# The second one-hot of the expert gates: four small ScalarE squares with the key as bias, where GpSimd subtracted and ScalarE squared once

## The reference, cut to what matters

```
v1, i1 = top_k(s[:, :, 0], 16);  v2, i2 = top_k(s[:, :, 1], 16)     # 8 heads, 128 keys on each side
vals, sel = top_k(v1[:, None] + v2[None, :], 16)
e1 = i1[sel // 16];  e2 = i2[sel % 16];  eid = e1 * 128 + e2         # 8 * 16 = 128 picks of a token
gate = softmax(vals)
w = gate * gelu(u[eid] . h);   y = sum over the picks of w * v[eid]
```

## Time and profile before

| | before |
|---|---|
| median of three runs | 2830.35 us (2830.07 to 2835.6) |
| profiled execution | 2832.78 us, of which the span of its instructions is 2831.2 us |
| mean granted clock of TensorE, whole span | 0.937 |
| gate loop of layer 0 | about 797.7 to 966.9 us, 169.2 us |
| gate loop of layer 1 | about 2227.5 to 2394.4 us, 166.9 us |
| VectorE busy in these loops | 160.24 and 161.08 us |
| ScalarE busy in these loops | 103.92 and 83.20 us |
| GpSimd busy in these loops | 77.41 and 76.91 us |
| granted clock in these loops | 0.94 and 0.80 |

### The profile page before, as it was taken

One profiled execution on the slowest core, in us unless ns is written; L12 is line 12 of the kernel. 1 busy time (PEld: TensorE's weight loads), 2 busy tenths in 40 slices (PEclk: granted clock), 3 DMA queues, 4 the chain that ended last, 5 costly groups with the idle time before them and its releaser, 6 DMA issues.

```text
span 2831.2 us, 55687 instructions
## 1 busy us (share of the span) xinstructions
PE 2554.8 (90%) x17972; PEld 2403.6 (85%) x17972; DVE 1794.1 (63%) x4076; ACT 1349.0 (48%) x2491; POOL 184.4 (7%) x201
## 2 busy tenths in 40 slices
PE   6986899999987899999796968999999867999996
PEld 3964899999965699999796858999999756999996
DVE  2435569884479755555546875588844798555554
ACT  2512445555556554545454223455556554555553
POOL 1000000000034200000000000000000243000000
PEclk7987999999999999999898878999999978999998
DMA  6444334444444354444342104344444200544442
GB/s 240 164 170 175 133 139 156 163 148 170 157 163 148 136 185 163 163 166 167 122 163 75 60 37 143 135 162 163 148 163 163 82 0 23 180 164 167 165 163 83
DMA packets 108412, 401.05 MB, mean 142 GB/s; under 512 B 12384, under 2 KB 12528, under 8 KB 107200
## 3 DMA queue, kind: packets, MB, share of 16 engines
q1 hardware_dynamic: 103104, 375.44, 37.9%
q0 software_dynamic: 5248, 24.88, 2.4%
HBM read 389.62 MB, written 10.65 MB: 141 GB/s over the span
## 4 chain that ended last, share of the span: by engine, by line
PE 79%; DVE 14%; issue 3%; DMA 2%; ACT 1%; DVEq 1%; SPq 0%; POOL 0%; ACTq 0%; POOLq 0%
PE ps L1186 22%; PE ps L1188 22%; PE ps L1187 22%; PE ps L1412 4%; DVE onehot L1092 3%; DMA raw<-in_ada_w 2%; PE ps L1215 1%; DVE spl L662 1%; PE ps L1332 1%; DVE big L1098 1%; PE ps L1348 1%; PE ps L1361 1%; DVE big L834 1%; PE ps L1251 1%; DVE big L1043 1%
## 5 line engine op out<-in xcount | busy, mean ns | idle before, releaser
L1186 PE MATMUL ps<-hs,spl 128*128 128x288 f32 x4960 | 1480.7, 299 | 78.3 <-DVE hs L714 46.0
L1187 PE MATMUL ps<-hs,spl 128*128 128x288 f32 x4960 | 1472.0, 297 | 0.0
L1188 PE MATMUL ps<-hs,spl 128*128 128x288 f32 x4960 | 1469.5, 296 | 0.0
L662 DVE TENSOR_TENSOR spl<-raw,spl 128x512 fp32r<-128x512 f32 x1240 | 843.4, 690 | 831.7 <-ACT spl L424 829.3
L424 ACT ACTIVATE spl<-raw 128x512 fp32r<-128x512 f32 x1240 | 772.9, 630 | 630.1 <-PE ps L1188 627.4
L1186 PEld LDWEIGHTS ps<-hs,spl 128*128 128x128 f32 x4960 | 939.0, 189 | 91.9 <-issue 60.5
L1188 PEld LDWEIGHTS ps<-hs,spl 128*128 128x128 f32 x4960 | 942.1, 190 | 0.0
L1187 PEld LDWEIGHTS ps<-hs,spl 128*128 128x128 f32 x4960 | 940.6, 190 | 0.0
L1412 PE MATMUL ps<-hs,onehot 128*128 128x128 f32 x1152 | 212.3, 333 | 91.1 <-DVE onehot L1092 65.6
L1412 PEld LDWEIGHTS ps<-hs,onehot 128*128 128x128 f32 x1152 | 175.3, 227 | 132.3 <-issue 58.2
L1092 DVE TENSOR_SCALAR onehot<-iota,choice 128x128 f32<-128x128 f32 x576 | 240.1, 480 | 5.5 <-PEq L1401 4.4
(11 more groups left out here) (223 smaller groups left out, 1282.5 us busy)
## 6 DMA issues: line engine op xcount, KB each, us to landing
raw<-in_peer_u SPq DMA_DIRECT2D x256, 512.0 KB, 3.2
raw<-in_peer_v SPq DMA_DIRECT2D x256, 512.0 KB, 3.2
raw<-in_ada_w SPq DMA_DIRECT2D x96, 512.0 KB, 5.2
raw<-in_peer_wq SPq DMA_DIRECT2D x32, 512.0 KB, 3.2
raw<-in_hg_w_in SPq DMA_DIRECT2D x32, 512.0 KB, 3.3
raw<-in_ab_w_in SPq DMA_DIRECT2D x28, 512.0 KB, 3.3
raw<-in_ab_w_out SPq DMA_DIRECT2D x8, 512.0 KB, 6.1
big<-in_state_hgrn POOLq DMA_DIRECT2D x8, 512.0 KB, 3.8
```

Of the source, the lines that this page charges most:

```text
L662: dve.tensor_tensor(spl[:, slot % 2, 1, cols], raw[:, slot, cols], spl[:, slot % 2, 0, cols].bitcast(F32), ALU.subtract).then_inc(low_read ...
L1186: pe.matmul(out, spl[:, slot, 0, cols], high, start=start, stop=False, skip_group_check=True)
L1187: pe.matmul(out, spl[:, slot, 0, cols], low, start=False, stop=False, skip_group_check=True)
L1188: return pe.matmul(out, spl[:, slot, 1, cols], high, start=False, stop=stop, skip_group_check=True)
```

## The change

ScalarE computes the square itself, from iota: Square(-1 * iota + e2), where e2 is the bias, one value for each partition. Since the bias belongs to one token, this is one 128 x 128 instruction for each token, four in place of one 128 x 512 instruction for each group. The subtraction on GpSimd goes, with the waits at its start (`choice_ready`, the last Gelu) and the semaphore `apart_ready`; ScalarE now waits for `choice_ready`. `apart` has three buffers in place of two, `seconds` lies behind it in the same memory, and the credit on `second_ready` becomes 3. ScalarE squares group g + 1 ahead of the Relu of group g, so its last iteration is written out behind the loop. VectorE's and TensorE's programs stay as they are, but for the 3.

```diff
-        apart, seconds = (hs[:].rearrange("p a b c -> p (a b c)")[:, 8 * P * w:8 * P * w + 8 * P].rearrange("p (s j e) -> p s j e", s=2, j=4)
-                          for w in range(2))
+        hs_flat = hs[:].rearrange("p a b c -> p (a b c)")
+        apart = hs_flat[:, 0:12 * P].rearrange("p (s j e) -> p s j e", s=3, j=4)
+        seconds = hs_flat[:, 12 * P:20 * P].rearrange("p (s j e) -> p s j e", s=2, j=4)
...
-                pool.wait_ge(choice_ready, l + 1)
-                pool.wait_ge(gelu_ready, EXP * (l + 1))
-                with pool.Fori(0, T // TOKENS) as i:
-                    for g in range(TOKENS // 4):
-                        n = i * (TOKENS // 4) + (T // 4 * l + g)
-                        pool.wait_ge(second_ready, n + 1)
-                        pool.tensor_tensor(apart[:, g % 2], iota[:, None, :].broadcast_to([P, 4, P]),
-                                           choice[:, 1, bass.ds(i * TOKENS + 4 * g, 4)][:, :, None].broadcast_to([P, 4, P]),
-                                           ALU.subtract).then_inc(apart_ready, 1)
...
+                act.wait_ge(choice_ready, l + 1)
+                groups, last = TOKENS // 4, T // TOKENS - 1
+
                 if l == 0:
-                    act.sem_inc(second_ready, 2)
-                with act.Fori(0, T // TOKENS) as i:
-                    for g in range(TOKENS // 4):
-                        n = i * (TOKENS // 4) + (T // 4 * l + g)
-                        act.wait_ge(apart_ready, n + 1)
-                        act.activation(apart[:, g % 2], apart[:, g % 2].bitcast(F32), ACT.Square).then_inc(apart_squared, 1)
-                        act.wait_ge(apart_squared, n + 1)
+                    act.sem_inc(second_ready, 3)
+
+                def squares(i, g):
+
+                    act.wait_ge(second_ready, i * groups + (T // 4 * l + g + 1))
+                    for j in range(4):
+                        ins = act.activation(apart[:, g % 3, j, :], iota[:], ACT.Square, scale=-1.0,
+                                             bias=choice[:, 1, bass.ds(i * TOKENS + (4 * g + j), 1)])
+                    ins.then_inc(apart_squared, 1)
+
+                def tokens(i, more):
+
+                    for g in range(groups):
+                        if g + 1 < groups:
+                            squares(i, g + 1)
+                        elif more:
+                            squares(i + 1, 0)
+                        act.wait_ge(apart_squared, i * groups + (T // 4 * l + g + 1))
                         act.wait_ge(onehot_free, i * TOKENS + (T * l + 4 * g + 4))
-                        act.activation(seconds[:, g % 2], apart[:, g % 2].bitcast(F32), ACT.Relu, bias=1.0, scale=-1.0).then_inc(second_ready, 1)
+                        act.activation(seconds[:, g % 2], apart[:, g % 3].bitcast(F32), ACT.Relu, bias=1.0, scale=-1.0).then_inc(second_ready, 1)
                         if l == 0:
                             if g in (2, 4):
                                 next_column(i + 12, g // 2 - 1, i * 4)
                             if g in (0, 2):
                                 next_row(i + 12, g // 2)
+                squares(0, 0)
+                with act.Fori(0, last) as i:
+                    tokens(i, True)
+                tokens(last, False)
...
-                                pe.wait_ge(second_ready, i * (TOKENS // 4) + (T // 4 * l + g + 1 + 2))
+                                pe.wait_ge(second_ready, i * (TOKENS // 4) + (T // 4 * l + g + 1 + 3))
```

More of the change, by code:

```diff
@@ L265, in trunk @@
         onehot_free = sem("onehot_free")
-        apart_ready, apart_squared = sem("apart_ready"), sem("apart_squared")
+        apart_squared = sem("apart_squared")
         gate_free = sem("gate_free")
```

## The result

The changed kernel takes 2812.93 us (median of 6 runs) against 2833.62 for the kernel before: a ratio of 0.9929, with a 95% interval of 0.9917 to 0.9942. It is 0.7% faster, by 21 us and not by the 53 of the forecast. The profiled execution took 2819.18 us, 13.6 less than that of the kernel before.

What follows compares the result with a forecast made beforehand. The prediction took VectorE to bound the two gate loops, its one-hots held up by GpSimd's subtraction. Savings of 41.4 us in layer 1 and 11.5 in layer 0 make 53, from the median 2830.35 to 2777 us; range 2760 to 2804.

Steps and rivals of the forecast that it cites:

- GpSimd's subtraction goes, VectorE's period falls to 1.62: In both gate loops, one-hots stand still while GpSimd subtracts; without it VectorE's group falls from 2.32 to 1.62 us.
- A Square starts 0.27 after the last: On ScalarE, each 128x128 Square with bias column starts 0.27 us after the last; four take 1.08 us.
- the 0.11 of the 10-element instructions: On ScalarE, 10-element instructions with bias column last 0.27 us, start 0.16 apart and so overlap by 0.11.
- Layer 1 falls to 125.5 us: Layer 1's gate loop: 2.5 + 119.5 (72 groups at 1.66) + 0.5 + 3 for the clock; 41.4 us saved.
- Layer 0's iteration falls from 14.11 to 13.15 us: Layer 0's gate loop: 0.96 us saved in each of 12 iterations, 11.5 us in all.
- The ring: Layer 0's cycle of ScalarE and TensorE waiting for each other, with a group's four Squares on it three times; 13.15 us.
- Layer 0, where the conditioning fills TensorE's gaps, kept 0.94: Argument against TensorE staying at 1.2 GHz in layer 1: layer 0's clock was 0.94; a shorter period fills layer 1's gaps.
- past 1.48: Layer 0: the time of a group's four Squares beyond which ScalarE alone sets the iteration.
- 7.23 + 5 S: Layer 0's iteration in us where ScalarE alone sets it; S is the time of a group's four Squares, forecast 1.08.
- VectorE is not late anywhere on the ring: Layer 0: at 1.62 us a group, VectorE holds up no step of the iteration.
- The rivals: Squares don't overlap, up to 2868 (0.07); another engine sets layer 1, 2795 or 2802 (0.15); VectorE not freed, 2830 (0.03); larger gain, 2759 (0.08).
- one, for layer 1 and as a constant 1.2 GHz: Smaller gain: TensorE stays at 1.2 GHz in layer 1, 24 us saved there, 2795 in all; chance 0.15 with slower Squares.

## Why the prediction was wrong

- **GpSimd's subtraction goes, VectorE's period falls to 1.62:** right. One-hots 344 ns, and back to 450 with a subtraction that nobody reads.
- **A Square starts 0.27 after the last:** close; 0.293 measured. The duration of 0.39 was right (0.388), but only 0.094 of it is overlapped; I had taken the 0.11 of the 10-element instructions, and averaged with an estimate that was smaller still, 0.26. From the formula of the Trainium skill (ScalarE: Activation LUTs, section "What ACT_TABLE_LOAD costs") I estimate 387 ns for 128 elements with a pointer bias, and starts 0.29 us apart. The trace agrees, with a median of 387 ns and (864.05 - 862.88) / 4 = 0.29.
- **Layer 1 falls to 125.5 us:** right, 126.4, with a group at 1.69 on ScalarE (from Relu to Relu, 2260.01 to 2261.70 us) and 1.62 on VectorE (from apply to apply, 2262.81 to 2264.43), and a clock of 0.91. The closeness is in part luck: the sum took 1.66 for the pace, and 3 us for the clock. With one product in layer 0's gaps the same loop took 124.3 us at a clock of 0.96, which puts the clock's share nearer 2 us.
- **Layer 0's iteration falls from 14.11 to 13.15 us:** this is the step that failed. The ring itself was nearly right, 13.47 at full clock. But I let it run at full clock throughout: the sum has no term for the clock in layer 0, and I asked about it only in layer 1. The changed ring loses 3.57 us to the half clock in eight of its iterations, and the loop 196.4 - 161.9 = 34.5 us, so that 11.5 us saved became 27.2 lost. "Layer 0, where the conditioning fills TensorE's gaps, kept 0.94" took the clock of the kernel before for that of another ring: there TensorE's products waited 68 times for VectorE or ScalarE (up to 960 us), at most 0.7 us; here 50 times for the Relu, up to 1.4 us.
- **Where ScalarE alone would set the ring:** the prediction's "past 1.48" should be 1.34, where its 7.23 + 5 S meets the ring's 13.15 + 3 (S - 1.08). No forecast used the 1.48.
- **VectorE is not late anywhere on the ring:** right; it waits 73 us for TensorE.
- **The rivals:** none of them is what happened. The clock was in one, for layer 1 and as a constant 1.2 GHz; it came in layer 0 and in a part of each iteration.

The sum with what was measured: 40.5 saved and 27.2 lost, 13.3 between the profiled executions. The medians differ by 20.7. The remaining 7 us are the choice of executions: the profiled one of the changed kernel was the slowest of its six, 6.3 above their median, and that of the kernel before lay 0.8 below its own. Single executions differ by that much ahead of the change already: the start of layer 0's loop lies between 791.6 and 803.6 us in those shown here.

## What to carry to other kernels

When an edit moves the pace of a loop from one engine to another, redo the waits of TensorE in the new order and ask for its clock there; the clock of the old loop did not carry over. Work that a ring waits for belongs into the ring's own wait: moving the Squares to where ScalarE stood idle was worth 1.5%, with the clock that it held, more than twice the change itself. Before an instruction is split into smaller ones, take the distance from start to start of the nearest one with the same operands, since that and not its duration is what is paid four times.

## What the runs showed of the hardware

- A VectorE one-hot of 344 ns on average goes to 450 (where nobody waits for the subtraction) or 480 (the kernel before) when GpSimd subtracts beside it once a group.
- TensorE's clock fell to 1.2 GHz with waits of 1.1 to 1.4 us in a ring of 13.5 us (it held in the second iteration, with the same waits), and held at 2.4 GHz in one of 12.0 us that had a wait of 1.38 us too. Products of constant tiles hold it as well: 36 of them won 34 us.
- Once it had fallen, the loop stayed in step with it: eight iterations in a row of 17.0 to 17.1 us, each with the fall and the rise at the same place.
- A bias column adds 0.09 us to a ScalarE instruction and to the distance to the next, whether its address is fixed or new for each.
